# Half of the heads' attention between the other half's projections and the output projection, in three attention mixers

## The reference

```python
def mixer_a(h, w_qkv, rel_bias, w_o):          # 16 heads of 64
    q, k, v = jnp.split(h @ w_qkv, 3, axis=-1)
    ...
        s = jnp.einsum('bqhd,bkhd->bhqk', qc, kb).astype(jnp.float32) * scale + bias
        s = jnp.where(valid, s, NEG_INF)
        p = jax.nn.softmax(s, axis=-1).astype(vb.dtype)
        return jnp.einsum('bhqk,bkhd->bqhd', p, vb)
    ...
    return o @ w_o

def mixer_c(h, w_qkv, lam, subln_g, w_o, lambda_init):     # 8 heads, each two softmaxes
    ...
        p = jax.nn.softmax(s, axis=-1)
        a = p[:, 0] - lam_full * p[:, 1]
        return jnp.einsum('bhqk,bkhe->bqhe', a.astype(v.dtype), v)
    ...
    o = rms_norm(o, subln_g) * (1.0 - lambda_init)
    return o.reshape(B, S, D) @ w_o
```

## Time and profile before

| | us |
|---|---|
| median of 3 runs | 3618.48 |
| lowest, highest | 3614.11, 3620.97 |
| profiled execution, first to last instruction | 3616.2 |
| PE busy in it | 3412.2 (94%) |
| DVE busy | 1876.4 (52%) |
| ACT busy | 1484.9 (41%) |
| POOL busy | 55.3 (2%) |

### The profile page before, as it was taken

The page is one execution under the profiler, slowest core; times in us unless marked ns, Lnnn a source line. Parts: engine busy times, 40 slices in busy tenths (PEclk is TensorE's granted clock), DMA queues, the critical chain, the costliest instruction groups (busy, mean ns, idle before and its releaser), DMA issues.

```text
span 3616.2 us, 53551 instructions
## 1 busy us (share of the span) xinstructions
PE 3412.2 (94%) x22679; PEld 3120.4 (86%) x22679; DVE 1876.4 (52%) x2599; ACT 1484.9 (41%) x2285; POOL 55.3 (2%) x132
## 2 busy tenths in 40 slices
PE   8999999999999998999999999989889999888899
PEld 8987998988989896999987998976689998667797
DVE  5454555555545455555554555564555447544554
ACT  4444444444444343444443444233344443333443
POOL 0000000000000000000000000000000000000000
PEclk9996999999999986999996999885799998768999
DMA  6561554554545541555561456440235564212353
GB/s 219 190 198 47 168 184 162 193 179 156 179 167 187 180 152 36 169 186 166 190 194 57 158 186 178 144 130 12 82 128 164 186 183 155 69 35 94 117 187 140
DMA packets 434402, 533.95 MB, mean 148 GB/s; under 512 B 27330, under 2 KB 398452, under 8 KB 434164
## 3 DMA queue, kind: packets, MB, share of 16 engines
q1 hardware_dynamic: 421220, 512.22, 43.3%
q10 hardware_dynamic: 12944, 18.31, 1.6%
HBM read 528.33 MB, written 1.11 MB: 146 GB/s over the span
## 4 chain that ended last, share of the span: by engine, by line
PE 89%; DVE 5%; ACT 3%; issue 1%; DMA 1%; POOL 1%; SPq 0%; ACTq 0%; DVEq 0%; POOLq 0%
PE bank L632 86%; PE bank L793 3%; ACT sb_prT L1027 1%; DVE sb_hT_low L1488 1%; DMA sb_slot<-in_w_in_dram 1%; POOL sb_rstd L1337 1%; DVE sb_low L1409 0%; PE bank L670 0%; ACT sb_hT_high L989 0%; ACT sb_high L1016 0%; DVE sb_oT_low L1490 0%; ACT sb_oT_high L989 0%; DVE sb_tmp L1698 0%; DMA sb_o_rows<-in_mem_dram 0%; DVE sb_x L1461 0%
## 5 line engine op out<-in xcount | busy, mean ns | idle before, releaser
L1409 DVE TENSOR_TENSOR sb_low<-sb_slot,sb_high 128x2048 fp32r<-128x2048 f32 (+1 forms) x480 | 1094.4, 2283 | 723.4 <-ACT sb_high L1016 722.9
L632 PE MATMUL bank<-sb_hT_high,sb_high 128*128 128x256 f32 x4264 | 1213.0, 284 | 22.4 <-DVE sb_hT_low L1488 17.1
L632 PE MATMUL bank<-sb_hT_low,sb_high 128*128 128x256 f32 x4264 | 1209.4, 284 | 0.0
L632 PE MATMUL bank<-sb_hT_high,sb_low 128*128 128x256 f32 x4264 | 1209.1, 284 | 0.0
L1016 ACT ACTIVATE sb_high<-sb_slot 128x2048 fp32r<-128x2048 f32 (+1 forms) x480 | 912.1, 1905 | 688.3 <-PE bank L632 596.6
L632 PEld LDWEIGHTS bank<-sb_hT_high,sb_high 128*128 128x128 f32 x4264 | 820.4, 192 | 26.4 <-DVE sb_hT_low L1488 17.2
L632 PEld LDWEIGHTS bank<-sb_hT_low,sb_high 128*128 128x128 f32 x4264 | 820.5, 192 | 0.0
L632 PEld LDWEIGHTS bank<-sb_hT_high,sb_low 128*128 128x128 f32 x4264 | 820.1, 192 | 0.0
L1067 ACT ACTIVATE sb_prT<-bank 128x256 f32<-128x256 f32 x220 | 84.5, 384 | 698.1 <-PE bank L632 698.1
L632 PE MATMUL bank<-sb_low,sb_hidden_high 128*128 128x512 f32 x880 | 350.2, 398 | 0.0
L632 PE MATMUL bank<-sb_high,sb_hidden_high 128*128 128x512 f32 x880 | 347.1, 394 | 0.0
(11 more groups left out here) (200 smaller groups left out, 3608.8 us busy)
## 6 DMA issues: line engine op xcount, KB each, us to landing
sb_slot<-in_ff_w_in_dram SPq DMA_DIRECT2D x176, 1024.0 KB, 5.2
sb_slot<-in_ff_w_out_dram SPq DMA_DIRECT2D x88, 1024.0 KB, 5.0
sb_slot<-in_w_gate_up_dram SPq DMA_DIRECT2D x44, 1024.0 KB, 5.2
sb_slot<-in_w_in_dram SPq DMA_DIRECT2D x42, 1024.0 KB, 5.3
sb_slot<-in_a_w_qkv_dram SPq DMA_DIRECT2D x24, 1024.0 KB, 5.2
sb_slot<-in_w_down_dram SPq DMA_DIRECT2D x22, 1024.0 KB, 5.0
sb_slot<-in_c_w_qkv_dram SPq DMA_DIRECT2D x12, 1024.0 KB, 5.2
sb_slot<-in_a_w_o_dram SPq DMA_DIRECT2D x8, 1024.0 KB, 5.2
```

The source lines that it names most:

```text
L632: return nc.tensor.matmul(o, lhsT, rhs, start=start, stop=stop)
L1409: V.tensor_tensor(low[i][:, 0:size], slots[n % SLOTS][:, 0:size], high[i][:, 0:size].bitcast(F32), ALU.subtract) \
```

## The change

In A and C mixers the order of heads, gemms and banks changes.
- Chunks arrive as v, v, then q and k of the first half of the heads (`in` 0 and 2), then of the second (1, 3). PE runs the v gemms, then qk 0 and 2, then `attention`.
- The 32 units now go by half first: half 0 for t = 0 (units 0 to 7), half 0 for t = 1 (8 to 15), half 1 for t = 0 (16 to 23), half 1 for t = 1 (24 to 31).
- After each step's scores, PE takes one piece of a generator `beside_attention`. Steps 0 to 15: the gemms qk 1 and 3, in pieces of 12 matmuls 256 wide. Steps 16 to 33: `oT` of (t, half) = (0, 0), (1, 0), (0, 1), and for each of them its share of the output gemm in four pieces of 6 matmuls 512 wide; two steps with no matmul piece stand at each turn of heads (16 and 17, 22 and 23, 28 and 29). The last quarter, (1, 1), comes behind attention.
- ACT and DVE take their part at the head of each iteration: weight splits in iterations 0, 4, 8, 12, 16, 26 and 28, evacuations of qk, and the high and low part of the turned heads.
- Banks: one for sums (0), one for transposed weights (1), two for scores (2, 3), four for the gemms (4 to 7).
- C norms its heads by quarters (`normed_heads`), with four powers of 128x4.
- In all four mixers and in the second block's two `branches` stages, the output weights come in four chunks of two k tiles by 1024 columns; in the B mixer and the two branches `wide_gemm` replaces `output_gemm`.

```diff
-        for c in (2, 3, 0, 1) if kind == 1 else range(w[win].shape[2] // 512):
+        for c in (2, 3, 0, 1) if kind == 1 else (4, 5, 0, 2, 1, 3):
...
-        for c in range(2):
-            cols((("mix", i), "out", c), w[wo][j], c * 512, 512)
+        rows((("mix", i), "out"), w[wo][j], 2)
...
+        MIX_SUMMED, MIX_TURNED, MIX_SCORES, MIX_DENSE = (Banks(psum, which, owner, taken, readers) for which in
+                                                         ((0,), (1,), (2, 3), (4, 5, 6, 7)))
...
                 for i in range(len(units) + 3):
+                    if second_half and i == len(units) // 2:
+                        second_half()
                     if i < len(units):
                         u = units[i]
-                        bank = SCORES.take(pe, (st, "s", i))
+                        bank = scores.take(pe, (st, "s", i))
...
+                    next(between, None)
                     if 2 <= i <= len(units) + 1:
...
-                        bank = TB.take(pe, (st, "p", i - 2))
+                        bank = turned_to.take(pe, (st, "p", i - 2))
...
-                    for c in range(4):
-                        columns_gemm([(st, "in", c, h) for h in range(2)], (st, "qk", c), hT)
...
-                    attention(st)
-                output_columns(st, KD)
-                output_gemm(st, [(st, "out", c, h) for c in range(2) for h in range(2)], oT)
+                    for c in (0, 2):
+                        columns_gemm([(st, "in", c, h) for h in range(2)], (st, "qk", c), hT)
...
+                    attention(st, MIX_SCORES, MIX_TURNED, MIX_SUMMED, beside_attention(st), lambda: heads_ready(st, 3))
+                    turn_heads(st, 1, 1, MIX_TURNED)
+                    for _ in output_steps(st, 1, 1):
+                        pass
...
+            def beside_attention(st):
+
+                for c in (1, 3):
+                    yield from columns_steps([(st, "in", c, h) for h in range(2)], (st, "qk", c), hT)
+                for t, hf, pool in ((0, 0, TB), (1, 0, TB), (0, 1, MIX_SCORES)):
+                    turn_heads(st, t, hf, pool)
+                    yield
+                    yield
+                    yield from output_steps(st, t, hf)
...
+            def normed_heads(st, t, hf):
...
+                step(V.tensor_tensor(xn[:, t, half], o_rows[:, t, half], o_rows[:, t, half], ALU.mult))
+                step(V.tensor_reduce(mean_sq[:, c0:c0 + 4], xn[:, t, half].rearrange("p (h d) -> p h d", h=4), AX.X, ALU.add))
...
+                dve.wait_ge(rstd_ready.sem, rstd_ready.at((st, "subln", t, hf)))
+                step(V.tensor_tensor(o4, o4, spread(rstd[:, c0:c0 + 4], P), ALU.mult))
```

More of the change, by code:

```diff
@@ L188, in weight_chunks @@
         rows((*L, "mla"), w["w_branch_mla_2"][l], 2)
-        for c in range(2):
-            cols((*L, "out", c), w["w_out_2"][l], c * 512, 512)
+        rows((*L, "out"), w["w_out_2"][l], 2)
         cols((*L, "xq"), w["w_xq_2"][l], 0, 512)
@@ L459, in output @@
         def output(st, t, h):
[L462 removed]
+            key = ((st, "y"), t, h)
             return (SB, TB)[t].of(key), key
@@ L940, in branches @@
                 awaited.extend(((st, "mT"), b) for b in range(KD // 2))
-                output_gemm(st, [(*L, "out", c, h) for c in range(2) for h in range(2)], oT)
+                wide_gemm("out", [(*L, "out", m) for m in range(4)], (st, "y"), oT)
             def memory(st):
@@ L1251, in branches @@
                 columns((st, "mT"), None, lambda k: oT[:, k, :])
-                for c, h in ((0, 0), (0, 1), (1, 0)):
-                    ahead((*L, "out", c, h))
+                for m in range(3):
+                    ahead((*L, "out", m))
                 turn(st)
@@ L1369, in _ @@
                     step(ins, "distances")
-                    power((st, "subln"), 0, 16)
+                    for hf in range(2):
+                        for t in range(NT):
+                            power((st, "subln", t, hf), 4 * (2 * t + hf), 4)
                 if kind == "l2":
@@ L1683, in mixer @@
+                    for c in (0, 2):
+                        for j in (1, 3):
+                            ahead((st, "in", c, j // 2))
+                            head_columns(st, c, j)
+                    attention(st, even(st, 8, 0) if i % 3 == 0 else differential(st), beside_attention(st))
+                    turned_heads(st, 1, 1)
+                    turn(st)
+                    return
                 columns((st, "oT"), None, lambda k: oT[:, k, :])
-                for c, h in ((0, 0), (0, 1), (1, 0)):
-                    ahead((st, "out", c, h))
+                for m in range(3):
+                    ahead((st, "out", m))
```

208 lines of the change are left out of this document (155 added, 53 removed).

## The result

The change makes the kernel a little slower. The medians are 3619.2 us before and 3630.9 us after. The ratio is 1.0039, with a 95% interval of 1.0027 to 1.0051; it matches 3630.9 against 3616.7, the median of the more numerous runs of before that stand beside the first experiments. The profiled execution of after has a span of 3629.5 us, 13.3 more than before. The forecast of 3589 had the wrong sign; its range reached up to 3645.

The account below looks back on a forecast made before the run. PE at half clock was taken to bound attention. Winning 10.5, 10.5 and 12.1 us in mixers 0, 3 and C and losing 3.5 in B and the branches gave 29.6 us, so 3589 us, range 3540 to 3645.

Parts of the forecast that it names:

- Part 1: Mixer 0's attention: gemm matmuls in the steps hold the clock at 1.00, so PE's attention work becomes 31.8 us.
- Part 2: PE's work in mixer 0 from first scores to next norm: 78.8 us against 114.0 before, 35 won if nothing waited.
- Part 3: PE's waits in mixer 0's attention, from splits ahead of the unit's work: 17.5 us, bounds 0 and 35.
- the chain: In attention, copy, split, scaling, exponential and copy in sequence on ACT and DVE: 6.7 us for 256 keys.
- rival A: Splits in attention hide: 12 of 17.5 us of waits gone, clock costs nothing; about 3540 us, chance 0.19.
- Part 4: End of mixer 0's attention: 3.2 us, plus 4.0 us in all for clock falls, bounds 0 and 10.
- Rival C: Clock falls at each long wait, needs several steps to return: 8 to 10 us more per mixer, 3616, chance 0.13.
- it takes little to keep the clock: From the cross attention, where PE busy 6.63 of 8 us held 1.00; getting the clock back takes much.
- Rival B: Clock falls at step 16 and stays low to attention's end: 23 us more in each mixer, 3658, chance 0.16.
- Part 5: C mixer: 119.7 us against 131.8, 12.1 won; the 13.00 us hole gives back only about a third.
- Part 6: B mixer and two branches: wide output gemm waits 2.05 us more, saves 0.9; 3.5 us lost in all.

Follow-up runs that it names:

- the first experiments: Earliest follow-up runs, each compared with the kernel before on the same chip; the kernel before had a median of 3616.7 us beside them.
- e3: e1 with the weight splits inside attention moved behind the unit's own work, DVE's half one iteration after ACT's; 3588.4 us, ratio 0.9918.
- e12: e3 with C's third turn later and output work held back, B's output wide by pairs, branches narrow, splits of iterations 16 and 28 behind turned heads; 3559.6 us.
- e1: Changed kernel with DVE's table wait and memset (mixers 0, 3) and distances block (mixer 2) put back behind qk 0's splits and copies; 3620.0 us, ratio 1.0004.
- e8: e3 with one of its seven splits, that of iteration 16, put back in front of the unit's own work on ACT and DVE; 3593.2 us, ratio 0.9931.
- e2: Kernel before with only its six output projections (four mixers, two branches) in the wide form; 3633.5 us, ratio 1.0047.
- e5: e3 with the output projection of the B mixer and two branches back in the narrow form of the kernel before; 3579.0 us, ratio 0.9892.

## Why the prediction was wrong

**Part 1, the clock, was right.** The granted clock is 1.00 from the first scores of after to 314 us, and PE was at 0.50 throughout before. Steps without a wait take 2.3 us with 128 keys and 2.5 to 2.9 with 256, against 2.2 and 2.7 forecast. e3 and e12 confirm it with 1.00 over 40 us and 0.96 over 94. That the 64 rows of the scores kept the clock low before is not shown: the transposes and weighted sums of the same stretch use 128, and no run changed that.

**Part 2, the work of 78.8 us**, was some 6 too low: 107.7 us measured in mixer 0, less 14.1 of waits behind the first scores and at most 8.6 of clock (0.08 of 108 us), leaves 85.0. e12 gives the same at a higher clock: 92.6, less 4.2 and 3.7, is 84.7. Which of the terms was too small is open.

**Part 3, the chain, was right in its places and somewhat high in its sizes.** Forecast 2.0, 1.8, 1.4, 1.4 at iterations 4, 8, 12, 26; measured 1.26, 1.23, 0.68, 1.30. At 16 forecast 4.3, measured 3.59; at 28 forecast 4.0, measured 2.24 and 0.75. In all 11.6 us, forecast 17.5, which rules out rival A, by which 5.5 would be left. e3 took the waits for the copy away and kept all seven splits, so their place in the order was the cause. What I didn't draw from my own chain is that the same lines written a few rows lower cost 31 us less.

**Part 4, the ends**: the tail was 2.5 us (3.2 forecast). The clock was the mis-sized term: by the stretches above, 0.08, 0.18 and 0.14 of their lengths, 8.6, 24 and 16 us, where I had 4, 5 and 4. These are upper readings, for a slow clock in a wait costs nothing; over PE's busy time alone they are 7.5, 19 and 14. They are read from one profiled run, no experiment changes the clock alone, and e1 shows that about the same waits can go with 0.92 or 0.86 in mixer 0. Rival C named this, at 8 to 10 us more for each mixer, and had 0.13. The step that failed is the sentence that it takes little to keep the clock, and with it the 4 us. The clock fell three times in mixer 0, behind the waits of 3.59 and 2.24 us and in the tail; it also fell behind 3.17 us ahead of attention and, in the kernels with the wide form, behind 2.08 in the cross attention. Rival B, a clock that stays low to the end of attention once it has fallen, is wrong in mixer 0 (its 2.6 us of gemm in a slow step is 2.8 by its own rates, 6 x 0.230 doubled, which changes nothing): the windows of after read 0.50 at 318 to 322 us and 0.98 from 322 to 350. In C it has a part: behind the wait of 3.31 us the clock reads 0.50 until 1432 us, while PE is busy all but 0.4 us from 1418 on. That is some 8 us of C's clock term in one stretch.

```profile
267.00:314.00 47.00, 42.61 (x294) 36.61 (x294) 23.62 (x43) 23.33 (x56) 0.00 (x0) 1.00 0.32 109
...
318.00:322.00 4.00, 4.00 (x13) 3.09 (x12) 0.58 (x2) 1.52 (x6) 0.00 (x0) 0.50 0.33 114
322.00:350.00 28.00, 23.17 (x111) 16.68 (x110) 13.53 (x27) 12.22 (x34) 0.00 (x0) 0.98 0.13 41
...
1420.00:1430.00 10.00, 9.77 (x27) 6.86 (x27) 3.75 (x10) 3.25 (x11) 0.00 (x0) 0.50 0.30 102
```

The Trainium skill (TensorE: Matmul & The Clock Gate, A second HAM failure mode) describes a clock that swings between its levels where PE idles briefly and often between groups of matmuls. The rows above agree in part: the clock does fall and return, but behind waits of 2 to 3.6 us, and not behind all of these, while the waits of 0.68 to 1.26 us in the first 47 us left the clock at 1.00. e8, as far as its 6 us can tell, does not give the fall a price beyond the wait itself.

**Part 5, the C mixer**, was forecast to win 12.1 us and lost 0.8 (132.6 against 131.8). The last gap is 6.18 + 1.41 us where I had 8.6 with evacuation, and all waits come to 25.5 us where I had 34.4. The work left over is 83.1 us (forecast 80.3). The loss against the forecast is the clock, up to 24 us where I had 5.

**Part 6** failed in two steps. The price of the wide form, 1.15 us a place, stands against 1.7 to 3.3 that e2 measured in the mixers, since the clock's part was missing, and the cross attentions behind the branches, 3.7 us, were not in the sum. And "the order of chunks, the DMAs and SP's queue cost nothing" meets no wait of after in the three things that it names, but leaves out a fourth, DVE's queue: the table's block was moved past the weight splits. This is the step that was left out. I followed what each moved line does on PE and SP, not on DVE.

**The sum.** Forecast -29.6, measured +13.3 us, 43 apart. Ahead of attention 4.9 + 5.2 + 4.6 = 14.7 (e1 gave back 12.7). In the mixers from the first scores on, measured against forecast, 4.2 + 12.9 + 7.0 = 24.1, nearly all of it clock and work that wasn't priced, by the readings above. The wide form and the cross attentions 2.1 more than counted. The rest, about 2, is scatter of the feed-forward stages, which last 191.8 to 193.9 us each in the profiled runs.

## What to carry to other kernels

When work is interleaved with a pipeline of several engines, put the foreign piece behind the pipeline's own instruction on each engine. Here the same seven splits cost 31 us more in front than behind and one iteration apart on the two engines; which of the two did it wasn't separated. When a stage's order is changed, go through every engine's queue and ask what each instruction now stands in front of, also those that the diff doesn't touch. What waits at the end of a pipeline can be covered by work kept back for it: 5.8 us in C, where 7.6 us of waits stood, nothing in the A mixers, where 2.5 stood.

## What the runs showed of the hardware

In attention alone (scores on 64 rows, transposes, weighted sums) PE stayed at a granted clock of 0.50 for 57 us while busy all the time; with twelve gemm matmuls in each step the same units ran at 1.00. The first cross attention was 1.3 to 1.7 us longer in every kernel whose stage before ended with 512 wide matmuls (and weights cut to match) in place of 256 wide ones. Behind the same wait of 2.1 us its clock read 0.69 over 5.5 us in those ten and 1.00 in the other four; the cause is open. POOL's power of 4 columns took 1.01 us, against 2.91 for 16 and 0.56 for one, so it pays for columns beside a fixed part:

```profile
1440.95 1.01 POOL L1443 TENSOR_TENSOR sb_rstd<-sb_mean_sq,sb_minus_half 128x4 f32<-128x4 f32 x1 [25.99 <-DVE sb_mean_sq L1695]
```

And one kernel's time follows its mean clock: of e1's eleven runs the fastest has a span of 3609.2 us at 0.930, the profiled one 3623.8 us at 0.925. Mixer 3, with the same code and the same waits, read 0.90 in e3 and 0.96 in e5, and was 6.4 us shorter. A difference of a few us between two stages of single profiled runs can be that and no more.
